# Interleaving the two output tiles of a pair in the order of TensorE's three products

## The reference

```python
def squared_relu_mlp(h, w1, w2):       # d = 1024, d_ff = 4096
    a = jax.nn.relu(h @ w1)
    return (a * a) @ w2
x = x + squared_relu_mlp(rms_norm(x, ff_norm_g[i]), w_ff1[i], w_ff2[i])
```

## Time and profile before

| | us |
|---|---|
| median of 3 runs | 4127.63 (4126.83 to 4133.5) |
| the profiled execution | 4127.1 |
| its span, first to last instruction | 4125.1 |
| TensorE busy | 3757.5 (91%) |
| TensorE weight loads busy | 2878.2 (70%) |
| VectorE busy | 2186.1 (53%) |
| ScalarE busy | 1293.1 (31%) |
| mean granted TensorE clock | 0.929 of full speed |

### The profile page before, as it was taken

The page is one execution under the profiler, slowest core; times in us unless marked ns, Lnnn a source line. Parts: engine busy times, 40 slices in busy tenths (PEclk is TensorE's granted clock), DMA queues, the critical chain, the costliest instruction groups (busy, mean ns, idle before and its releaser), DMA issues.

```text
span 4125.1 us, 42083 instructions
## 1 busy us (share of the span) xinstructions
PE 3757.5 (91%) x17374; PEld 2878.2 (70%) x17374; DVE 2186.1 (53%) x3927; ACT 1293.1 (31%) x2131; POOL 42.7 (1%) x52
## 2 busy tenths in 40 slices
PE   7767989999988999999986988999999889889999
PEld 6423668887843667887764966788888747667886
DVE  5655458884768457884434145433333552454344
ACT  4243333233435333333212121332322221223332
POOL 0000000000000000000000000000000000000000
PEclk9889999999989999999998956999999999669999
DMA  5100215542222114542201100111111201002231
GB/s 181 58 0 11 72 41 181 176 153 82 72 62 51 61 51 143 181 166 86 80 21 32 52 1 1 61 63 62 62 62 43 83 21 52 31 22 82 93 101 62
DMA packets 241643, 300.41 MB, mean 73 GB/s; under 512 B 37928, under 2 KB 193194, under 8 KB 241324
## 3 DMA queue, kind: packets, MB, share of 16 engines
q1 hardware_dynamic: 228396, 247.39, 18.8%
q0 software_dynamic: 13056, 50.33, 3.5%
HBM read 295.60 MB, written 4.00 MB: 73 GB/s over the span
## 4 chain that ended last, share of the span: by engine, by line
PE 78%; DVE 15%; ACT 5%; issue 1%; DMA 0%; SPq 0%; DVEq 0%; ACTq 0%
PE ps L94 77%; DVE t L115 6%; ACT t L100 5%; DVE t L107 4%; DVE t L121 1%; DVE t L111 1%; DVE ps L107 1%; DVE ps L115 1%; DVE ps L112 1%; PE ps L97 1%; DVE t L118 0%; DMA t<-in_mem 0%; DVE t L127 0%; ACT L100 0%; DMA t<-in_ctx 0%
## 5 line engine op out<-in xcount | busy, mean ns | idle before, releaser
L94 PE MATMUL ps<-t,t 128*128 128x512 f32 (+6 forms) x16766 | 3652.0, 384 | 331.6 <-DVE t L107 119.4
L94 PEld LDWEIGHTS ps<-t,t 128*128 128x128 f32 (+3 forms) x16766 | 2799.3, 197 | 1130.1 <-issue 245.8
L100 ACT ACTIVATE t<-t 128x1024 fp32r<-128x1024 f32 (+8 forms) x1207 | 853.8, 740 | 1424.4 <-PE ps L94 920.4
L107 DVE TENSOR_TENSOR t<-t,t 128x1024 fp32r<-128x1024 f32 (+6 forms) x878 | 786.6, 919 | 716.7 <-ACT t L100 700.4
L100 ACT ACTIVATE t<-ps 128x512 f32<-128x512 f32 (+4 forms) x510 | 262.9, 537 | 1119.3 <-PE ps L94 1022.5
L115 DVE SCALAR_TENSOR_TENSOR t<-t,t,t 128x256 f32<-128x256 f32 (+4 forms) x951 | 448.0, 536 | 7.4 <-ACT t L100 1.2
L107 DVE TENSOR_TENSOR t<-ps,t 128x512 f32<-128x512 f32 (+4 forms) x308 | 197.9, 664 | 390.0 <-PE ps L94 295.1
L115 DVE SCALAR_TENSOR_TENSOR t<-ps,t,t 128x512 f32<-128x512 f32 (+1 forms) x220 | 133.6, 659 | 265.7 <-PE ps L94 265.4
L118 DVE COPY t<-ps 128x256 f32<-128x256 f32 (+1 forms) x169 | 78.2, 492 | 286.5 <-PE ps L94 267.8
L100 ACT ACTIVATE t<-ps,t 128x512 f32<-128x512 f32 (+3 forms) x151 | 92.4, 618 | 139.8 <-PE ps L94 69.8
L97 PEld LDWEIGHTS ps<-t,t 128*128 128x128 f32 x544 | 69.1, 153 | 86.4 <-issue 57.1
(11 more groups left out here) (21 smaller groups left out, 209.3 us busy)
## 6 DMA issues: line engine op xcount, KB each, us to landing
t<-in_w_ff SPq DMA_DIRECT2D x64, 1024.0 KB, 7.4
t<-in_w_mlp SPq DMA_DIRECT2D x64, 1024.0 KB, 5.2
t<-in_ada_w POOLq DMA_DIRECT2D x48, 1024.0 KB, 5.7
t<-in_w_in SPq DMA_DIRECT2D x30, 1024.0 KB, 5.3
t<-in_w_qkv_o SPq DMA_DIRECT2D x12, 1024.0 KB, 5.1
t<-in_w_mem_kv SPq DMA_DIRECT2D x8, 1024.0 KB, 6.4
t<-in_w_mem_q SPq DMA_DIRECT2D x8, 1024.0 KB, 5.0
t<-in_w_mem_o SPq DMA_DIRECT2D x8, 1024.0 KB, 5.1
```

Of the source, the lines that this page charges most:

```text
L94: return Issued(self, self.e and self.e.matmul(o, l, r, start=start, stop=stop, skip_group_check=True))
L100: return Issued(self, self.e and self.e.activation(o, i, f, **kw))
L107: return Issued(self, self.e and self.e.tensor_tensor(o, a, b, op))
```

## The change

In `feature` the loops over the tiles of the pair and over the three products are exchanged. For each contraction tile the kernel now does product 1 of t0, product 1 of t1, product 2 of t0, and so on. The same matmuls with the same operands run. The two banks alternate, and the weights change at each matmul of a single-view product.

```diff
                 for kk in range(u.kc):
                     for label in ready_k(kk):
                         pe.wait_ge(*label)
-                    for t in pair:
-                        for (a, b) in TERMS:
-                            first, last = kk == 0 and (a, b) == (0, 0), kk == u.kc - 1 and (a, b) == (1, 0)
+                    for (a, b) in TERMS:
+                        first, last = kk == 0 and (a, b) == (0, 0), kk == u.kc - 1 and (a, b) == (1, 0)
+                        for t in pair:
                             for v in t.views:
                                 if first and v.opens:
                                     opening(v.bank)
```

## The result

| | before | changed |
|---|---|---|
| median (9 runs each) | 4127.47 us | 4138.43 us |
| lowest to highest | 4125.33 to 4133.5 | 4137.99 to 4142.53 |
| ratio, 95% interval | 1 | 1.0028 (1.0017 to 1.0038) |
| span of the profiled execution | 4125.1 us | 4136.0 us |

The changed kernel is slower by 10.96 us, where 10.3 us were forecast (4137.5 us), and its span by 10.9 us. The page hardly shows it. Busy times, slices and chain are as the earlier trace rows, and only TensorE's idle time before line 94 has grown, from 331.6 to 336.6 us, and the busy time by 6 us. A matmul is recorded with 0.39 us in the stream and with 0.47 to 0.50 us after a stop, longer than the distance to the next start, so the records cover short waits.

What follows compares the result with a forecast made beforehand. TensorE, busy 3757.5 of 4125.1 us, was taken as the bound. Later t0 (5.6 + 0.9), t1's bank (3.5) and retention (0.3) sum to 10.3 us, giving 4137.5 us; own range 4133.5 to 4141.5, full range 4129 to 4145 us.

Steps and rivals of the forecast that it cites:

- Rate: Matmul stream everywhere: alternating banks and weights leave the spacing at 0.2322 us, so 0, between -1 and +1 us.
- One sign of being wrong: Last MLP: any spacing other than 0.232 us would show that the rate does depend on neighbours.
- that rule's condition: Rival, slower stream: small stops lower the clock, 115 us more, 4243 us; chance 0.08, shared with more stops.
- t0 ends later: First block's MLPs: t0 ends 0.464 us later, lengthening 12 stops by 5.6 us and two third uses by 0.9 us.
- C: Third use of a four-use MLP cycle: late weights start it 0.27 us later, swallowed by the next use's stop; uncovered, 3.3 us.
- the idle time before D: First MLP, TensorE's stop before the fourth use of each four-use cycle: to grow from 0.34 to about 0.8 us.
- a second stop of about 0.2 us: First MLP: a new TensorE stop one matmul behind the one that ends each cycle's known stop.
- t1's bank: Start of each cycle's fourth use: second matmul waits for VectorE's second add, 12 x 0.29 = 3.5 us, from 2.4 to 4.8.
- Retention: Second layer's last gate product: ScalarE's activations end later before the factors TensorE awaits, 0.3 us, between 0.2 and 0.46.
- Hidden places: Before norms and attentions: waits for square buffers cover t0's later end, 0; if the norms' buffer were free, 3.4 us.
- The sum: Whole kernel: 5.6 + 0.9 + 3.5 + 0.3 = 10.3 us slower, 4137.5 us; chance 0.64.

Runs made afterwards that it cites:

- e1: Against the kernel before, products alternate between the tiles at all contraction tiles but the first and last of each pair: 4127.38 us, ratio 0.9999.
- e5: The changed order everywhere but in the first block's MLPs, which keep the order of the kernel before: 4127.52 us, ratio 1.0002.
- e6: The order of the kernel before, but in single-view pairs t1's first product moves ahead of all of t0's: 4133.74 us, ratio 1.0016.
- e3: Against the kernel before, products alternate only at the last contraction tile, so t0 ends two matmuls later: 4133.25 us, ratio 1.0014.
- e8: Against the kernel before, t0's third product and t1's first change places at the last contraction tile, t0 ending one matmul later: 4130.38 us, ratio 1.0011.
- e2: Against the kernel before, products alternate only at the first contraction tile, so the second matmul opens t1's bank: 4130.38 us, ratio 1.0007.
- e4: Kernel before, but single-view pairs with 8 contraction tiles do the last two for t0, then t1; t0 ends 3 matmuls earlier: 4119.47 us, ratio 0.9979.
- e7: Changed kernel, but single-view pairs with 8 contraction tiles do the last two for t0, then t1: 4121.74 us, ratio 0.9988 against the kernel before.

## Why the prediction was right

**Rate: 0, right for the order.** e1 alternates in all inner contraction tiles and costs 0.07 us. The two-view stream kept 0.3510 us a couple. One sign of being wrong did appear, another spacing than 0.232 us in the last MLP (0.2333), but e5 with the same order there has 0.2324, so neighbours are not its cause. The clock in the windows of the MLPs stayed at 1.00 with alternating banks. The Trainium skill ("TensorE: Matmul & The Clock Gate", "A second HAM failure mode: psum-queue depth-cycling") tells of a kernel that cycles through PSUM banks and in which TensorE's short idle times between groups of matmuls let the clock gate oscillate. The prediction took the banks alone as that rule's condition. Here they alternate without idle times, and even e6 with its stops of 0.94 us every 49.2 us had clock 1.00 in the first MLP, so no run here shows that oscillation.

**t0 ends later: 5.6 + 0.9 us, right.** From the second to the last use of both MLPs that runs beside a modulate step the traces give +6.5 us in e3 and +3.2 us in e8 for both layers together, and 14 times 0.464 and 0.232 is 6.5 and 3.2. The chain was read rightly: ScalarE is held by t0's end, not by t1's.

**C: swallowed, right in the sum, wrong in the picture.** C starts 0.25 us late (0.27 forecast; it started 0.05 us after its weights' end, where 0.08 were counted), and D's growth is then only the remainder. I wrote that the idle time before D would grow from 0.34 to about 0.8 us. It grew to 0.49, because what TensorE waits before C it no longer waits before D. Likewise "a second stop of about 0.2 us" is recorded as 0.03 us of idle time, since the restarting matmul's record is longer. The distance of the starts, 0.50 for 0.30 us, has it.

**t1's bank: 3.5 us, right.** The fourth matmul of D started 1.07 us after the first and not 0.77: 0.30 us, for 0.29 forecast. Inside it two small errors cancel, which is luck: the second matmul started at 0.51 us and not at 0.53, and the third followed it at 0.34 us and not at 0.30. e2 alone gives 0.32 us a cycle.

**Retention: 0.3 us, measured 0.25.** **Hidden places: 0, right,** with ScalarE's square at the same distance from the product's end to 0.01 us.

**The sum.** In the traces both MLPs together are 10.0 us longer (5.6 + 3.5 + 0.9 = 10.0 by the steps), the retention 0.25, and the last MLP 1.4 by a stream that runs at 0.2333 us. The medians differ by 10.96, with an interval from 7.0 to 15.7, so the last us is not told apart from the spread. That the totals agree to 0.7 us is partly luck, since stages elsewhere in the changed kernel's trace gained or lost up to 2.6 us as the clock fell at other moments (last section). The steps are shown by the cycles, not by the total.

## What to carry to other kernels

Before work is reordered inside a unit whose length stays the same, ask who waits for its first part: here the same matmuls, at a rate that the order did not change, cost 11 us, or gained 8, only by when the first of two tiles ended and when the second's bank was asked for. Where the chain from an input to what the bound engine waits for has no gap, as here from B's t0 through ScalarE and VectorE to D, 0.46 us on that input comes out as 0.46 us of waiting each time. The chain of waits names which of the two tiles holds it. Finish first what another engine needs first, and open a bank late when the engine that frees it is behind. Where nobody waited, as before the norms and in the last MLP, the order was no matter.

## What the runs showed of the hardware

**One stream, two spacings.** Single-view matmuls of 512 columns at clock 1.00 follow each other in one of two patterns. In one, single spacings run from 227 to 242 ns with a mean of 232.4, in the other 229 and 238 alternate, mean 233.3. In each trace a stretch of 1,440 matmuls of the last MLP had one of them throughout. Windows of 305 us in that MLP, first e5, whose order alternates, then e3, whose order doesn't but in the last contraction tile:

```profile
3765.00:4070.00 305.00, 305.00 (x1314) 247.34 (x1313) 122.28 (x138) 108.83 (x146) 0.00 (x0) 1.00 0.29 94
3765.00:4070.00 305.00, 305.00 (x1309) 245.39 (x1308) 119.56 (x135) 109.27 (x147) 0.00 (x0) 1.00 0.29 93
```

Before, e2, e4, e5, e6 and e7 had the first, changed, e1, e3 and e8 the second. The changed kernel and e5 have the same order in this MLP and differ, so the order there doesn't choose it. What does stays open, and with one trace of each kernel it isn't known whether a kernel keeps its pattern from one execution to the next; it is worth 0.4% of such a stretch. Both means are above the 216 ns that the Trainium skill's formula gives for 512 columns ("TensorE: Matmul & The Clock Gate", "Back-to-back issue gap"). That section calls the formula the gap of isolated matmuls and gives about 131 ns for a stream of weight loads and matmuls of 512 columns, which is further still from the 232 to 233 ns here.

**The clock moves the ends.** In the trace the clock was at half speed for 587 us in all before, 595 us in the changed kernel, and from 584 to 605 us in the others. The changed kernel's lag, 11.7 us soon after the second MLP's last stop, was between 8 and 12 us at later places and 10.7 us at the end. Single stages gain or lose up to 3.4 us with it: e3's trace is that much longer between 2100 and 2220 us of the kernel before, with 6.8 us more at half speed. Between 3170 and 3442 us the traces of changed, e2, e3, e4, e5 and e8 are 2.5 to 2.6 us longer, with 6.8 us more at half speed, and those of e1, e6 and e7 are not. That follows neither the changed order nor the sign of the shift (e4 is earlier, e3 later), so it is best read as where the work happens to lie against the moments at which the clock changes. No run separates that from other causes.
